# Second parts of the feed-forward "out" chunks, made on GpSimd instead of VectorE

## What is computed

```python
def swiglu(x, w_in, w_out):                        # stages ffn1 and ffn2 of the first block
    gate, up = jnp.split(x @ w_in, 2, axis=-1)
    return (jax.nn.silu(gate) * up) @ w_out

def conv_glu(hn, w_in, conv_w, conv_b, w_out):     # stages conv0 and conv1 of the second block
    u, gate_in = jnp.split(hn @ w_in, 2, axis=-1)
    c = (conv_w[0] * shift_right(gate_in, 2) + conv_w[1] * shift_right(gate_in, 1)
         + conv_w[2] * gate_in + conv_b)
    return (jax.nn.gelu(c, approximate=False) * u) @ w_out
```

## Time and profile before

| | |
|---|---|
| median of three runs | 1288.86 us |
| the profiled execution, its own time | 1288.69 us |
| its span, first to last instruction | 1286.9 us |
| TensorE busy | 1272.6 us (99%) |
| VectorE busy | 981.0 us (76%) |
| ScalarE busy | 698.9 us (54%) |
| GpSimd busy | 94.0 us (7%) |
| granted TensorE clock | 0.998 |

### The profile page before, as it was taken

The page is one execution under the profiler, slowest core; times in us unless marked ns, Lnnn a source line. Parts: engine busy times, 40 slices in busy tenths (PEclk is TensorE's granted clock), DMA queues, the critical chain, the costliest instruction groups (busy, mean ns, idle before and its releaser), DMA issues.

```text
span 1286.9 us, 26185 instructions
## 1 busy us (share of the span) xinstructions
PE 1272.6 (99%) x10976; PEld 1213.3 (94%) x10976; DVE 981.0 (76%) x1286; ACT 698.9 (54%) x843; POOL 94.0 (7%) x107
## 2 busy tenths in 40 slices
PE   9999999999999999999999999999999999999998
PEld 8999999999999999999999999999999889999998
DVE  5877767689878777678775587977887767988777
ACT  5544544475546555554635654455465675445545
POOL 0000000122000000002130200000000160000000
PEclk9999999999999999999999999999999999999999
DMA  9555574544355555543430045555554505555540
GB/s 366 210 197 196 196 245 164 201 135 162 132 195 188 202 201 196 196 165 111 175 132 4 2 180 181 197 197 199 200 176 140 197 2 197 196 196 196 197 163 33
DMA packets 34912, 219.15 MB, mean 170 GB/s; under 512 B 4411, under 2 KB 6884, under 8 KB 9612
## 3 DMA queue, kind: packets, MB, share of 16 engines
q1 hardware_dynamic: 32032, 215.62, 47.4%
q10 hardware_dynamic: 2796, 2.31, 0.6%
HBM read 216.72 MB, written 1.06 MB: 169 GB/s over the span
## 4 chain that ended last, share of the span: by engine, by line
PE 86%; DVE 8%; ACT 2%; issue 2%; DMA 1%; POOL 0%; SPq 0%; POOLq 0%; ACTq 0%; DVEq 0%
PE ps L990 20%; PE ps L996 16%; PE ps L1050 15%; PE ps L1001 9%; PE ps L953 2%; DVE weights_second_parts L2721 2%; PE ps L1684 2%; PE ps L1172 2%; PE ps L1132 2%; PE ps L1315 2%; PE ps L933 2%; PE ps L959 1%; PE ps L1725 1%; PE ps L1504 1%; PE ps L1513 1%
## 5 line engine op out<-in xcount | busy, mean ns | idle before, releaser
L2721 DVE TENSOR_TENSOR weights_second_parts<-weight_bays,weights_first_parts 128x2048 fp32r<-128x2048 f32 x130 | 296.4, 2288 | 87.5 <-ACT weights_first_parts L1908 87.4
L1908 ACT ACTIVATE weights_first_parts<-weight_bays 128x2048 fp32r<-128x2048 f32 x130 | 247.5, 1908 | 34.9 <-PE ps L990 18.4
L996 PE MATMUL ps<-x_both_parts,weights_first_parts 128*128 128x512 f32 x1024 | 242.3, 380 | 0.0
L996 PEld LDWEIGHTS ps<-x_both_parts,weights_first_parts 128*128 128x128 f32 x1024 | 184.3, 190 | 20.3
L1001 PEld LDWEIGHTS ps<-x_both_parts,weights_second_parts 128*128 128x128 f32 x1024 | 134.0, 191 | 8.8 <-DVE weights_second_parts L2721 2.1
L1050 PE MATMUL ps<-hidden_first_part,weights_first_parts 128*128 128x256 f32 x704 | 136.4, 276 | 0.0
L1001 PE MATMUL ps<-x_both_parts,weights_second_parts 128*128 128x256 f32 x1024 | 135.3, 275 | 0.9 <-DVE weights_second_parts L2721 0.9
L1050 PE MATMUL ps<-hidden_second_part,weights_first_parts 128*128 128x256 f32 x704 | 133.5, 275 | 0.0
L1050 PE MATMUL ps<-hidden_first_part,weights_second_parts 128*128 128x256 f32 x704 | 131.7, 275 | 0.0
L1915 ACT ACTIVATE arena<-ps 128x512 f32<-128x512 f32 x64 | 38.2, 597 | 158.7 <-PE ps L1001 158.5
L990 PE MATMUL ps<-x_both_parts,weights_first_parts 128*128 128x256 f32 x896 | 110.5, 277 | 0.0
(11 more groups left out here) (511 smaller groups left out, 2489.8 us busy)
## 6 DMA issues: line engine op xcount, KB each, us to landing
weight_bays<-in_conv_in SPq DMA_DIRECT2D x44, 1024.0 KB, 4.8
weight_bays<-in_ffn_in SPq DMA_DIRECT2D x42, 1024.0 KB, 4.8
weight_bays<-in_ffn_out SPq DMA_DIRECT2D x22, 1024.0 KB, 4.7
weight_bays<-in_conv_out SPq DMA_DIRECT2D x22, 1024.0 KB, 4.7
weight_bays<-in_mix_in SPq DMA_DIRECT2D x19, 1024.0 KB, 4.9
weight_bays<-in_hyb_in SPq DMA_DIRECT2D x13, 1024.0 KB, 5.0
weight_bays<-in_ple_gate SPq DMA_DIRECT2D x12, 1024.0 KB, 4.8
weight_bays<-in_mix_out SPq DMA_DIRECT2D x4, 1024.0 KB, 5.0
```

The lines of the kernel that those rows point to most:

```text
L996: nc.tensor.matmul(dst, hi[:, k, j * P:(j + 1) * P], x_parts[:, :, k].rearrange("p c (a b) -> p c b a", a=2), start=(k == 0), stop=False, ...
L1908: nc.scalar.activation(hi, raw, ACT.Copy).then_inc(*w_hi_ready.inc(f, g, kind, of - g))
L2721: v.tensor_tensor(lo, raw, hi, ALU.subtract).then_inc(*w_lo_d.inc(f, g, kind, of - g))
```

## The change

The subtraction of the "out" chunks is taken out of VectorE's `rest_of_weights` and put into a function of GpSimd's own, with a loop of the same four rounds. GpSimd does the stage's `power` first, then out 0, the loop, and out 9 and out 10. It waits for ScalarE's first part and signals a new semaphore, `w_lo_g`, on which TensorE waits in place of `w_lo_d`. Gate and up chunks stay on VectorE.

```diff
@@ -428,6 +428,7 @@
         hid_lo_ready = signal("hidden_second_part_ready")
         w_hi_ready = signal("weights_first_part_ready")
         w_lo_d = signal("weights_second_part_by_vector")
+        w_lo_g = signal("weights_second_part_by_gpsimd")
         x_hi_a = signal("x_first_part_by_scalar")
         x_lo_d = signal("x_second_part_by_vector")
         acc_ready = signal("projection_ready")
@@ -1059,11 +1060,11 @@
                         for tile in range(KD):
                             add(tile, 0, hi, hid_hi)
                             add(tile, 1, hi, hid_lo)
-                        wait_split(pe, (w_lo_d,), f, "out", g, i)
+                        wait_split(pe, (w_lo_g,), f, "out", g, i)
                         for tile in range(KD):
                             mm = add(tile, 2, lo, hid_hi)
                     elif g == GROUPS - 1:
-                        wait_split(pe, (w_lo_d,), f, "out", g, i)
+                        wait_split(pe, (w_lo_g,), f, "out", g, i)
                         for q in range(PAIRS):
                             for tile in (2 * q, 2 * q + 1):
                                 add(tile, 0, hi, hid_hi)
@@ -2484,6 +2485,24 @@
                 c = slice(at, at + width)
                 nc.gpsimd.tensor_tensor(rstd[:, c], msq[:, c], minus_half[:, c], ALU.pow).then_inc(*rstd_ready.inc(*n))
 
+            def ffn(f):
+
+                def group(g, i=None):
+                    for kind, of in split_steps(g):
+                        if kind == "out":
+                            raw, hi, lo = split_views(f, kind, of)
+                            pool.wait_ge(*w_hi_ready.at_group(i, f, g, kind, of - g))
+                            nc.gpsimd.tensor_tensor(lo, raw, hi, ALU.subtract).then_inc(*w_lo_g.inc(f, g, kind, of - g))
+
+                power(f)
+                group(1)
+                with pool.Fori(0, ROUNDS) as i:
+                    since = w_lo_g.count
+                    group(2, i)
+                    group(3, i)
+                    w_lo_g.repeated(f, since, ROUNDS)
+                group(GROUPS - 1)
+
             def mix1():
 
                 pool.wait_ge(*x_lo_d.at("mix1", PAIRS - 1))
@@ -2562,22 +2581,22 @@
                         ins = nc.gpsimd.tensor_scalar(s, s, mden[:, hd % 6, n:n + 1], None, ALU.mult)
                     ins.then_inc(*mla_g.inc("probs", hd))
 
-            power("ffn1")
+            ffn("ffn1")
             power("mix1")
             mix1()
             power("rec", width=8)
-            power("ffn2")
+            ffn("ffn2")
             power("ple1")
             power("hyb", width=4)
             power("ple20", "e", at=6)
             hyb()
-            power("conv0")
+            ffn("conv0")
             power("ple20")
             power("mla")
             power("ple21", "e", at=6)
             power("latent", width=4)
             mla()
-            power("conv1")
+            ffn("conv1")
             power("ple21")
             power("all")
 
@@ -2716,6 +2735,8 @@
 
             def rest_of_weights(f, g, i=None, which=slice(0, None)):
                 for kind, of in split_steps(g)[which]:
+                    if kind == "out":
+                        continue
                     raw, hi, lo = split_views(f, kind, of)
                     dve.wait_ge(*w_hi_ready.at_group(i, f, g, kind, of - g))
                     v.tensor_tensor(lo, raw, hi, ALU.subtract).then_inc(*w_lo_d.inc(f, g, kind, of - g))
```

## The result

The changed kernel takes 1304.26 us (median of 1302.02, 1303.94, 1304.58 and 1307.32) against 1288.73 for the kernel before on the same chip: a ratio of 1.0118, 95% interval 1.0106 to 1.0130, so +15.5 us where +6.1 was forecast and +11.3 was the end of the range. The profiled execution is the shortest of the four, 1302.02 us with a span of 1300.3, which is 13.4 us more than the span before.

A forecast was written before the change was run, and what follows sets the result against it. TensorE was taken as the bound (1272.6 of 1286.9 us busy). Start waits of 3.0 (ffn1), 2.3 (ffn2) and 0.8 (both convolution stages), loops and ends nothing, gave 1288.69 + 6.1 = 1294.8 us; range 1289.5 to 1300.

The forecast's parts named there:

- the starts: First chunks of each feed-forward stage: TensorE waits while GpSimd holds VectorE, +3.0 us ffn1, +2.3 ffn2, +0.4 each convolution stage.
- VectorE isn't held: Rival: VectorE isn't held, or GpSimd is at the floor; starts lose nothing, 0.9 us of waits go, 1287.8; chance 0.11.
- order at the start: Rival: in ffn1 VectorE's hidden second part goes before GpSimd's subtraction; the 3.0 us go, 1291.8; chance 0.07.
- GpSimd is slower than 4.42 us: Rival: longer subtractions make the convolution loops exceed TensorE's period, up to 16 us per us above, and starts grow; chance 0.20.
- 1305 at 5.0 us: The slower-GpSimd rival's sum for 5.0 us subtractions: starts 3.9 + 4.0 + 2 x 2.2, plus loops; about 1305 us.
- I take 4.1.: Duration of one 128x2048 subtraction on GpSimd, taken as 4.1 us from four 128x512 ones of 1.04 us.
- the sign that the prediction had named for being too low: A GpSimd duration above 4.4 us, or TensorE waiting in every convolution round, would make the prediction too low.
- upper bound of 4.16: Four undisturbed 128x512 GpSimd instructions of 1.04 us, as the upper end for one 128x2048 subtraction.
- Cost nothing, as long as the subtraction is under 4.42.: Loops: GpSimd's hold of VectorE fits idle time below 4.42 us; TensorE wants out with 2.5 us to spare.
- 16 x 0.08 at 4.5: Slower-GpSimd rival's loop cost for 4.5 us subtractions: 0.08 us in each of 8 groups x 2 convolution stages.
- Ends. Nothing.: Stage ends: GpSimd finishes chunks 9 and 10 at 937.5, just before the tap sum at 937.67; no cost.
- floor of 2.288 us: Least GpSimd subtraction time, VectorE's own; the sum with it: +1.2 in ffn1, 0.9 of waits go, 1289.0.

The follow-up runs named there:

- the extra subtraction: Kernel before, VectorE's work unchanged; in ffn1 GpSimd adds nine 128x2048 subtractions on columns nothing else uses: 1292.53 us against 1289.35.
- the run with chunks 1 to 8: Of the changed kernel's moved subtractions only those of out chunks 1 to 8 (32 of 44) go to GpSimd: 1294.04 us, +4.5 against the kernel before.
- the even chunks: Only out chunks 2, 4, 6 and 8 (16 subtractions of 44) go to GpSimd: 1289.68 us against 1289.35 for the kernel before.
- the run with chunks 9 and 10: Only out chunks 9 and 10 (8 subtractions of 44) go to GpSimd: 1291.33 us, +1.8 against the kernel before.
- the repeated kernel: The changed kernel run once more with no edit: 1304.10 us against 1289.35 for the kernel before.
- two such repairs: Changed kernel with each GpSimd subtraction cut in four: 1317.49 us; changed kernel with GpSimd's chunk 0 started behind VectorE's hidden second part: 1309.30 us.
- the run with chunk 0 alone: Only out chunk 0 of each feed-forward (4 subtractions of 44) goes to GpSimd: 1297.13 us against 1289.52 for the kernel before.
- the run in quarters: Changed kernel with each GpSimd subtraction of 128x2048 cut into four of 128x512: 1317.49 us, +28.0 against the kernel before.

## Why the prediction came out too low

**The sign and the mechanism** were right: the two engines take turns by whole instructions, GpSimd's subtraction is about twice as long, and TensorE waits at the starts of the stages. *VectorE isn't held* is refuted by the extra subtraction; *order at the start* didn't occur, and when it was brought about it cost more, so its 1291.8 was wrong as well. *GpSimd is slower than 4.42 us* had the duration right and what follows from it wrong: the loops cost nothing. That its 1305 at 5.0 us lies next to the measured 1304.26 is luck, since no subtraction that VectorE left alone took 5.0, and 4.3 of its 16.6 us came from the loops.

**"I take 4.1."** This term failed first, and with it came the sign that the prediction had named for being too low, a duration above 4.4. Undisturbed it is 4.53 to 4.57 us. The 1.04 us for 512 came from an instruction with a broadcast operand; the same shape with two full inputs takes 1.26 here. The upper bound of 4.16 was therefore no bound. Its working, with 4.55 put in: 3.4 in ffn1, 3.1 in ffn2, 1.3 in each convolution stage, 9.1 in place of 6.1. Measured at the starts: 3.48, 3.00 (1.40 + 0.26 + 1.34) and 1.89 twice (0.49 + 0.17 + 1.23), 10.3 less the 0.9 that were there before: 9.4. With the right duration the starts were right to 0.3 us. (The 4497 ns that the Trainium skill gives, page "GPSIMD Engine Reference", section "3.1 Elementwise — side-by-side cycle accounting", weighed in the prediction, was within 2% of the 4.53 to 4.57 us that the trace shows.)

**"Cost nothing, as long as the subtraction is under 4.42."** It is over, 4.68 to 4.69 in the loop of conv0, and behind chunk 1 TensorE still never waits there. GpSimd's subtractions in conv0's loop:

```profile
828.95 4.68 POOL L2495 TENSOR_TENSOR weights_second_parts<-weight_bays,weights_first_parts 128x2048 fp32r<-128x2048 f32 x1 [11.54 <-ACT weights_first_parts L1909]
844.57 4.68 POOL L2495 TENSOR_TENSOR weights_second_parts<-weight_bays,weights_first_parts 128x2048 fp32r<-128x2048 f32 x1 [10.94 <-ACT weights_first_parts L1909]
860.17 4.69 POOL L2495 TENSOR_TENSOR weights_second_parts<-weight_bays,weights_first_parts 128x2048 fp32r<-128x2048 f32 x1 [10.93 <-ACT weights_first_parts L1909]
```

They come every 15.61 us, less than TensorE's 15.84 a group: VectorE's chain is late once, at chunk 1, and then catches up. So the bound of 4.42 was too low, and the rival's extra 16 x 0.08 at 4.5 wasn't there. (By its own 2.5 us to spare, which the sum at 5.0 takes off, it shouldn't have been.) The loops themselves were right at nothing: the change and the run with chunks 1 to 8 have no wait behind chunk 1, and the even chunks agree.

**"Ends. Nothing."** Wrong by 1.1 us at the end of each convolution stage, 2.2 in all, shown alone by the run with chunks 9 and 10 (0.9 each there). Two steps meet here. With 4.55 the prediction's own rule gives 0.7 at each end: chunks 9 and 10, from 929.29, are done at 938.39, and the tap sum (L2780, two SBUF tensors, counted as held) was due at 937.67. The rest, some 0.4 by this estimate, comes from the first tap (L2776), which was left out of the held ones: the pair takes 2.24 and 1.86 us instead of 0.73 when GpSimd reads. The same section of the Trainium skill's page on SBUF ("SBUF — State Buffer", "Who interferes with whom") names `tensor_scalar` among the instructions that can enter a two-port mode and then contend with GpSimd; the hold agrees, though no run shows in which mode it ran. The prediction sorted by the number of SBUF tensors alone.

**What had no term.** A pass restarted after a wait is about 0.2 us longer (5.59 for 5.36): 1.7 us in TensorE's busy time. And behind a long wait the granted clock falls in some executions: nothing in the one profiled first, 1.7 us in the second, and the median stands 2.2 us above the shortest.

In sum: 6.1, +3.0 for the duration at the starts, +0.3 left over there, +2.2 for the ends, +1.7 for restarts = 13.3, the profiled execution (1302.02 - 1288.69 = 13.3). The duration alone, 6.1 + 3.0 + 2 x 0.7, would have given 1299.2, still inside the range that ended at 1300; the tap, the restarts and the clock, which had no term, took the time beyond it. The other three executions are longer by 1.9 to 5.3; that the clock is the cause there is not shown, only in the one execution of the repeated kernel.

Two slips change nothing above. The rival *VectorE isn't held* puts GpSimd at the floor of 2.288 us beside it at 1287.8, but the prediction's own sum for that floor is 1289.0. And GpSimd's smallest instruction is not the 0.106 us of the earlier trace rows: the trace has fills of 0.097.

## What to carry to other kernels

A free engine that shares a resource with a busy one isn't free: before moving work there, list which instructions of the other engine can't run beside it, and look at the places without slack, the first and last groups of a stage, since a steady loop can hide a hold that its edges can't (16 subtractions in the loops cost nothing, 4 at the starts cost 7.6 us). Price the moved instruction by a row with the same operands, not only the same shape. When a wait is moved by splitting or reordering, follow the whole queue of both engines behind it: two such repairs made this kernel 5 and 13 us slower.

## What the runs showed of the hardware that I had not expected

- Where VectorE leaves it alone, GpSimd's subtraction of 128x2048 takes 3.60 us with one buffer as both inputs and output, 4.53 with two different inputs, whether the output is f32 or fp32r.
- A `tensor_scalar` of VectorE with one SBUF tensor is held by a GpSimd subtraction (1.68 to 2.24 us for two, 0.73 undisturbed). A fill on GpSimd did not hold VectorE's subtraction (0.69 inside a fill of 1.82).
- GpSimd's instructions are held too (6.45 us for one of 4.55, 3.31 for one of 1.26), and by more than one instruction in a row: 9.24 us, with three of VectorE's ahead.
- After a wait of TensorE of about 3.5 us the granted clock came down from its upper to its lower level (0.50 in the windows from 39 to 42 us of the run with chunk 0 alone) in some executions of one and the same kernel, and stayed up in others; in the run in quarters it also came down behind a wait of 1.9 us (0.50 from 1277 to 1279).
